# Latent and cross attention by features: values as the held operand, probabilities scaled before they are turned

## The reference

```python
def causal_block_attention(q, k, v, scale):      # queries in blocks of 128
    s = einsum('bqhmd,bkhmd->bhmqk', q_blk, k) * scale     # masked by position
    p = softmax(s, axis=-1)
    return einsum('bhmqk,bkhd->bqhmd', p, v)

# latent: 8 heads, q and k of 96 features, v of 64; output 512 tokens x 512
y_mla = latent_attention(...) @ w_mla_o[l]
# cross: 4 heads of 128 features over 256 memory rows, no mask; output 512 x 512
y_mem = memory_cross_attention(xq, mem_n, ...) @ w_cross_o[l]
merged = gates[:, :, 0] * y_diff + gates[:, :, 1] * y_mla + gates[:, :, 2] * y_mem
x = x + merged @ w_out[l]
```

## Time and profile before

| | us |
|---|---|
| median of 3 runs (3521.92 to 3522.84) | 3522.53 |
| the profiled execution, its own time | 3525.09 |
| its span in the trace | 3523.8 |
| mean share of the TensorE clock granted | 0.981 |

### The profile page before, as it was taken

One profiled execution on the slowest core, in us unless ns is written; L12 is line 12 of the kernel. 1 busy time (PEld: TensorE's weight loads), 2 busy tenths in 40 slices (PEclk: granted clock), 3 DMA queues, 4 the chain that ended last, 5 costly groups with the idle time before them and its releaser, 6 DMA issues.

```text
span 3523.8 us, 53214 instructions
## 1 busy us (share of the span) xinstructions
PE 3367.1 (96%) x21944; PEld 2751.0 (78%) x21944; DVE 2067.1 (59%) x3837; ACT 1332.9 (38%) x2476; POOL 82.7 (2%) x60
## 2 busy tenths in 40 slices
PE   7989999999999999999999999999899989999998
PEld 6777788888888777788888888767677767788887
DVE  6776753554447776644644458655666579664344
ACT  4465543332225566443333223222333234232221
POOL 0000000000000000000000000000000035000000
PEclk9999999999999999999999999999899999999999
DMA  4221223333333221223333333324310324243332
GB/s 137 79 68 49 58 75 108 97 95 96 96 107 119 79 67 49 60 76 116 94 98 96 96 102 89 90 76 118 106 32 28 109 72 138 92 130 96 96 99 86
DMA packets 353816, 314.73 MB, mean 89 GB/s; under 512 B 11348, under 2 KB 281812, under 8 KB 353576
## 3 DMA queue, kind: packets, MB, share of 16 engines
q1 hardware_dynamic: 352712, 309.10, 29.4%
q10 hardware_dynamic: 864, 2.23, 0.2%
HBM read 287.69 MB, written 23.59 MB: 88 GB/s over the span
## 4 chain that ended last, share of the span: by engine, by line
PE 77%; DVE 14%; ACT 4%; issue 3%; DMA 1%; SPq 0%; POOL 0%; DVEq 0%; ACTq 0%; POOLq 0%
PE banks L528 13%; PE banks L530 12%; PE banks L529 12%; PE banks L427 9%; PE banks L429 8%; PE banks L428 8%; DVE weights_r L368 2%; PE banks L628 1%; PE banks L1100 1%; PE banks L1113 1%; ACT weights_high_r L361 1%; PE banks L1204 1%; PE banks L2375 1%; PE banks L2671 1%; PE banks L2610 1%
## 5 line engine op out<-in xcount | busy, mean ns | idle before, releaser
L368 DVE TENSOR_TENSOR weights_r<-weights,weights_high_r 128x1024 fp32r<-128x1024 f32 (+3 forms) x520 | 598.9, 1159 | 360.6 <-ACT weights_high_r L361 359.6
L528 PE MATMUL banks<-h_T_hi,weights_high_r 128*128 128x512 f32 (+2 forms) x1904 | 758.9, 399 | 16.6 <-DVE cellsB L3636 5.1
L530 PE MATMUL banks<-h_T_hi,weights_r 128*128 128x512 f32 (+2 forms) x1904 | 736.6, 387 | 0.0
L529 PE MATMUL banks<-h_T_lo,weights_high_r 128*128 128x512 f32 (+2 forms) x1904 | 736.0, 387 | 0.0
L361 ACT ACTIVATE weights_high_r<-weights 128x1024 fp32r<-128x1024 f32 (+3 forms) x520 | 510.7, 992 | 363.7 <-DMA weights<-in_w_mlp 214.0
L528 PEld LDWEIGHTS banks<-h_T_hi,weights_high_r 128*128 128x128 f32 x1904 | 361.1, 190 | 107.4 <-issue 33.8
L530 PEld LDWEIGHTS banks<-h_T_hi,weights_r 128*128 128x128 f32 x1904 | 360.7, 189 | 72.5
L529 PEld LDWEIGHTS banks<-h_T_lo,weights_high_r 128*128 128x128 f32 x1904 | 361.4, 190 | 69.9 <-issue 3.9
L427 PE MATMUL banks<-weights_high_r,h_T_hi 128*128 128x512 f32 (+3 forms) x704 | 291.8, 414 | 10.6 <-ACT cellsX L577 6.0
L429 PE MATMUL banks<-weights_high_r,h_T_lo 128*128 128x512 f32 (+3 forms) x704 | 267.1, 379 | 0.0
L428 PE MATMUL banks<-weights_r,h_T_hi 128*128 128x512 f32 (+3 forms) x704 | 266.7, 379 | 0.0
(11 more groups left out here) (568 smaller groups left out, 5373.2 us busy)
## 6 DMA issues: line engine op xcount, KB each, us to landing
weights<-in_w_in SPq DMA_DIRECT2D x182, 512.0 KB, 3.8
weights<-in_w_mlp SPq DMA_DIRECT2D x128, 512.0 KB, 3.8
weights<-in_ffn_w_in SPq DMA_DIRECT2D x44, 512.0 KB, 3.8
weights<-in_w_out SPq DMA_DIRECT2D x24, 512.0 KB, 3.6
weights<-in_ffn_w_down SPq DMA_DIRECT2D x22, 512.0 KB, 3.7
weights<-in_w_mem_kv SPq DMA_DIRECT2D x16, 512.0 KB, 3.6
weights<-in_w_diff_o SPq DMA_DIRECT2D x16, 512.0 KB, 3.5
weights<-in_w_mla_o SPq DMA_DIRECT2D x8, 512.0 KB, 3.4
```

Source lines behind the costliest of these rows:

```text
L368: ve.e.tensor_tensor(self.part(c.w_raw_r, u), self.part(c.w_raw, u), self.part(c.w_high_r, u).bitcast(F32), ALU.subtract).then_inc(*ve.tel ...
L528: pe.e.matmul(out, lhsT=wh[:, k, :], rhs=hi[k][:, cols], start=(k == 0), stop=False)
L529: pe.e.matmul(out, lhsT=wh[:, k, :], rhs=lo[k][:, cols], start=False, stop=False)
L530: mm = pe.e.matmul(out, lhsT=wl[:, k, :], rhs=hi[k][:, cols], start=False, stop=(k == self.chunks - 1))
```

## The change

`Attention` now makes its output features by tokens. DVE's reciprocal comes one place earlier in its step (before mask and maximum), ACT then scales the probabilities where they lie in SBUF (a new instruction, unit n-2), the transposes move from unit n-3 to n-4, and the values from n-4 to n-5. In the values product the values are held and the turned probabilities move. For `mla` two heads run together: head 2i writes partitions 0 to 63 of a bank, head 2i+1 partitions 64 to 127, each from 64 held columns, chunk by chunk in turn, and the units are reordered so that the two heads of a pair follow one another. A bank (5 or 7 in turn) collects four query blocks, 512 columns; then ACT copies it out as the high part and DVE subtracts for the low part, straight into the operands of the output projection. Scores have three banks (2 to 4) in place of four. `mla` keeps four turned probability tiles (cells C[0:4]) in place of two; the probabilities rotate over five tiles in place of four. `mo turn` and `xo turn` are gone, and what waited for them waits for `mla.done()` and `cross.done()`, whose marks are now DVE's low parts.

```diff
-    def __init__(self, c, tag, units, out, ready, free):
+    def __init__(self, c, tag, units, together, out, pT, ready, free):
...
+        self.all = together * NT
+        self.n = len(units) + 5
+    def values_pe(self, first):
+        c, pe = self.c, self.c.pe
+        f, block = first // self.all, first % self.all // self.together
+        if block == 0:
+            c.fill(self.tag, "values", f, bank=5 + 2 * (f % 2))
...
+        for j in range(chunks):
+            for e, (m, v) in enumerate(some):
+                dim = v[j].shape[-1]
+                mm = pe.e.matmul(bank[e * dim:(e + 1) * dim, block * P:(block + 1) * P], lhsT=v[j], rhs=self.turned(m)[:, j * P:(j + 1) * P],
+                                 start=(j == 0), stop=(j == chunks - 1))
     def pe(self):
...
+            if self.unit(n - 5) and (n - 4) % self.together == 0:
+                pe.wait_ge("emptied", self.tag, "turn", n - 5)
+                self.values_pe(n - 4 - self.together)
             if self.unit(n - 4):
...
-                    mm = pe.e.matmul(bank[:, 0:v[j].shape[-1]], lhsT=c.pT[n % 2][:, j * P:(j + 1) * P], rhs=v[j],
...
+                pe.wait_ge("scaled", self.tag, m)
...
-                bank = c.fill(self.tag, "scores", n, ring="scores")
+                bank = c.fill(self.tag, "scores", n, bank=2 + n % 3)
     def act(self):
...
+            if self.unit(n - 2):
+                m, st, p = n - 2, self.stat(n - 2), c.probs[(n - 2) % 5][:, 0:self.keys(n - 2)]
+                ac.wait_ge("inverse_sum", self.tag, m)
+                ac.wait_ge("exp", self.tag, m)
+                ac.e.activation(p, p, ACT.Copy, scale=st[:, 3:4]).then_inc(*ac.tell("scaled", self.tag, m))
...
-                ac.e.activation(dst, c.slots[(self.tag, "values", m)][:, 0:dst.shape[-1]], ACT.Copy,
-                                scale=self.stat(m)[:, 3:4]).then_inc(*ac.frees(self.tag, "values", m))
...
+            if f is not None:
+                ac.wait_ge("filled", self.tag, "values", f, NT - 1)
+                ac.wait_all(self.free)
+                ac.e.activation(self.out(f)[0], c.slots[(self.tag, "values", f)][:, :], ACT.Copy).then_inc(*ac.tell("turned_high", self.tag, f))
     def dve(self):
...
+            if f is not None:
+                hi, lo = self.out(f)
+                ve.wait_ge("turned_high", self.tag, f)
+                ve.wait_all(self.free)
+                ve.e.tensor_tensor(lo, c.slots[(self.tag, "values", f)][:, :], hi.bitcast(F32),
+                                   ALU.subtract).then_inc(*ve.frees(self.tag, "values", f))
...
-        mo = plain(C[0:4])
+        mo4 = two_parts(E[0:8:2], E[1:8:2])
-                   for h in range(MH) for b in range(NT)]
+                   for pair in range(MH // 2) for b in range(NT) for h in (2 * pair, 2 * pair + 1)]
-        mo_turn = turn("mo turn", mo, 4, P, pair_out(mo4), mla.done(), mla.done(), pair=True)
-        P_.beside(mo_turn, 183, 184.3)
-        xo_turn = turn("xo turn", xo, 4, P, pair_out(xo4), cross.done(), mla_out.done(), pair=True)
-        P_.beside(xo_turn, 284.5, 292)
```

More of the change, by code:

```diff
@@ L1090, in got, with ended, turned @@
         return self.c.slots[(self.tag, "scores", n)][:, 0:self.keys(n)]
+    def ended(self, n):
+        m = n - 5
+        return m // self.all if self.unit(m) and (m + 1) % self.all == 0 else None
+    def turned(self, n):
+        return self.pT[n % len(self.pT)]
+    def values_pe(self, first):
[3 more added lines that the diff above has]
+            c.fill(self.tag, "values", f, bank=5 + 2 * (f % 2))
+        bank = c.slots[(self.tag, "values", f)]
+        some = [(first + e, self.units[first + e][2]) for e in range(self.together)]
+        chunks = len(some[0][1])
+        for j in range(chunks):
[3 more added lines that the diff above has]
+                                 start=(j == 0), stop=(j == chunks - 1))
+        mm.then_inc(*pe.tell("filled", self.tag, "values", f, block))
     def pe(self):
@@ L1119, in act @@
         for n in range(self.n):
[L1120 to L1129 removed]
+            if self.unit(n - 2):
[3 more added lines that the diff above has]
+                ac.e.activation(p, p, ACT.Copy, scale=st[:, 3:4]).then_inc(*ac.tell("scaled", self.tag, m))
+            if self.unit(n - 4):
+                m, keys = n - 4, self.keys(n - 4)
                 ac.wait_ge("filled", self.tag, "turn", m)
[L1131 to L1133 removed]
+                before = m - len(self.pT)
+                if before >= 0:
+                    ac.wait_ge("filled", self.tag, "values", before // self.all, before % self.all // self.together)
+                ac.e.activation(self.turned(m)[:, 0:keys], c.slots[(self.tag, "turn", m)][:, 0:keys],
                                 ACT.Copy).then_inc(*ac.frees(self.tag, "turn", m))
@@ L1150, in dve @@
         for n in range(self.n):
+            if self.unit(n - 2):
+                m, st = n - 2, self.stat(n - 2)
+                ve.wait_ge("exp", self.tag, m)
+                ve.e.reciprocal(st[:, 3:4], st[:, 2:3]).then_inc(*ve.tell("inverse_sum", self.tag, m))
             if self.unit(n - 1):
@@ L1158, in dve @@
                 if m > 7:
-                    ve.wait_ge("emptied", self.tag, "values", m - 8)
+                    ve.wait_ge("scaled", self.tag, m - 8)
                 ve.e.tensor_reduce(st[:, 0:1], got, AX.X, ALU.max, negate=True).then_inc(*ve.tell("top", self.tag, m))
-            if self.unit(n - 2):
-                m, st = n - 2, self.stat(n - 2)
-                ve.wait_ge("exp", self.tag, m)
-                ve.e.reciprocal(st[:, 3:4], st[:, 2:3]).then_inc(*ve.tell("inverse_sum", self.tag, m))
+            f = self.ended(n)
+            if f is not None:
[4 more added lines that the diff above has]
+                                   ALU.subtract).then_inc(*ve.frees(self.tag, "values", f))
             yield
     def done(self):
-        return [("emptied", self.tag, "values", m) for m in range(max(0, len(self.units) - 4), len(self.units))]
+        return [("emptied", self.tag, "values", f) for f in range(len(self.units) // self.all)]
 class DifferenceAttention(Stage):
@@ L1818, in __init__ @@
         kB_turn = turn("kB turn", kB, 4, P, lambda h: kTB[h], kB_norm.done(), mla.done())
-        mo4 = two_parts(E[0:4], E[4:8])
-        mo_turn = turn("mo turn", mo, 4, P, pair_out(mo4), mla.done(), mla.done(), pair=True)
-        P_.beside(mo_turn, 183, 184.3)
         P_.beside(qB_turn, 183.8, 184)
@@ L1828, in __init__ @@
         bias = lambda n: G["b_gate"][:, n * KD:(n + 1) * KD]
-        mla_out = GatedBranch(c, tag("mla out"), mo4, 4, mo_turn.done(), gates(1), bias(1), i["w_mla_o"][l], merged, False,
-                              [*mo_turn.done(), *kB_turn.done(), *gains])
+        mla_out = GatedBranch(c, tag("mla out"), mo4, 4, mla.done(), gates(1), bias(1), i["w_mla_o"][l], merged, False,
+                              [*mla.done(), *kB_turn.done(), *gains])
         P_.products(*mla_out.jobs)
```

51 lines of the change are left out of this document (17 added, 34 removed).

## The result

The changed kernel takes 3550.07 us (median of 3 runs, 3545.69 to 3552.04) against 3522.53: the ratio is 1.0077, with a 95% interval of 1.0063 to 1.0090. It is 27.5 us slower, where the prediction had 10.8 us faster, and outside the range of 3501 to 3529. The profiled execution is the median one, with a span of 3548.5 us at a mean granted clock of 0.979.

The account below looks back on a forecast made before the run. PE, busy 96% of the span, was taken to bound the kernel. Terms of 1.8 + 1.7 + 1.2 + 1.3 - 0.6 = 5.4 us a layer, 10.8 for two, took 3522.5 to 3511.7 us, range 3501 to 3529.

Parts of the forecast that it names:

- What bounds the kernel: Whole kernel: PE, busy 96% of the span, so PE work removed is time won unless PE then waits.
- The two turns: Removing both turns' transposes from PE: 1.8 us gained for xo turn and 1.7 us net for mo turn, a layer.
- xo turn: Cross attention's turn: its 16 transposes come off PE whole, 1.8 us a layer.
- mo turn: Latent attention's turn: 3.1 us of work and waits gone, 1.4 us of new waits, net 1.7 us a layer.
- The values: Latent attention's values: column halves run at once, 16.0 less 8.8 less 5.6 us of excursions; 1.2 us gained a layer taken.
- B: Rival: loads of 64 held columns in the latent values are not hidden, 8 us more in all, 3519.7 us; chance 0.09.
- C: Rival: the latent values' column halves run in turn, that term becoming -7.2 us a layer, 3528.5 us; chance 0.07.
- The waits at kh1 turn: Where kh1 turn meets mla: the 0.86 us wait goes, the longer stays about the same; 1.3 us gained a layer.
- What is added on ACT and DVE: Scalings and low parts on ACT and DVE, mostly hidden: -0.6 us a layer, ends 0 and -16.
- Rival D: Scaling holds up ACT's copies: PE waits 1.0 us before each of 16 values groups a layer, 3542.5 us; chance 0.08.
- The clock: Sign of being wrong: a second half-clock stretch in the latent attention, about 1.7 us for each 3.4 us, in no case.
- The slack of the transposes: Attention pipeline: the transposes' two steps behind the exponential stay two; no PE cost.

Follow-up runs that it names:

- e4: The kernel before with the change applied to the cross attention alone, the latent attention and its turn left as before; 3515.9 us, ratio 0.9984.
- e9: e3 with DVE's reciprocal removed too, so neither scaling nor reciprocal, outputs of latent and cross attention unnormalised; 3516.3 us, ratio 0.9985 to the kernel before.
- e3: e1 without the scaling instruction and ACT's wait for the reciprocal, outputs of both attentions unnormalised; 3524.2 us, ratio 1.0007 to the kernel before.
- e1: The changed kernel with ACT's copy of the turned probabilities put ahead of the scaling; 3532.9 us, ratio 1.0029 to the kernel before.
- e11: The changed kernel with the scaling on GpSimd's queue and the reciprocal back behind mask and maximum; 3528.1 us, ratio 1.0016 to the kernel before.

## Why the prediction was wrong, point by point

**What bounds the kernel.** Right: PE's work and its waits, and nothing else, make the time. The waits were misjudged, not the bound.

**The two turns.** xo turn: right. Its 32 transposes (of the 64 that are gone) left no wait in the cross attention, and e4, with this term of 3.6 us alone, is 5 us faster (2 to 9). mo turn: forecast 1.7 us net a layer. The idle stretches behind the latent attention are 1.67 + 0.25 + 0.73 = 2.65 us where they were 1.87, so with 1.8 us of work gone the net is 1.0 us in layer 0. kB turn's wait for the low part is what was forecast (some 1.6, it is 1.67); the 0.3 us for shorter waits was too much.

**The values.** The mechanism was right and the size too small. Column halves run at once, 0.109 us for two. The excursion costs 0.25 us and not 0.35: the prediction took it from the row halves of the earlier trace rows, where it had the held operand loaded in the open, and here the loads are hidden. The term is 16.0 - 8.8 - 16 x 0.25 = 3.2 us a layer in place of 1.2. With the turns this makes 2 x (3.6 + 3.2) = 13.6 us of work. The account, with the clock taken out, has 15.3 for the changed kernel, 14.7 for e9 (16.4 less 1.7), 12.9 for e3 (17.1 us at the lower level) and 11.7 for e1 (23.9 us). Rivals B and C fall. The rule of the Trainium skill behind B (TensorE: Matmul & The Clock Gate, The mechanism) does not hold for these loads: held columns for one half were loaded while the other half, with the same rows, ran (at 331.02 us of the changed kernel both halves' passes begin, and the next loads of both begin 2 ns behind them).

**The waits at kh1 turn.** Forecast 1.3 us gained a layer. The stretch grew: 0.65 + 0.25 + 3.61 + 0.86 = 5.4 us in layer 0, where it was 2.26, and 4.4 in layer 1 (0.32, 0.25, 3.61, 0.24), where it was 2.64. The prediction had the late piece right, an exponential behind a weight split, and left its price "at about the same size". It asked what PE would wait for, not what ACT's queue now held ahead of it. The kernel before, at the same place, has the copy 0.1 us behind ACT's half of the split, and PE waits 0.43 us for it:

```profile
285.33 1.05 ACT L361 ACTIVATE weights_high_r<-weights 128x1024 fp32r<-128x1024 f32 x1
...
286.48 0.38 ACT L1133 ACTIVATE cellsS<-banks 128x256 f32<-128x256 f32 x1
...
286.91 0.66 PE L1100 MATMUL banks<-cellsM,cellsS 128*128 128x64 f32 x4 [0.43 <-ACT cellsS L1133]
```

After, it stands behind DVE's half too, through the reciprocal.

**What is added on ACT and DVE: the step that failed.** The term was -0.6 us a layer, and measured it is about -16 (half of the 32 us between after and e9; in the first part of the two accounts alone, -13). The prediction had named -16 as this term's far end and left it out of its range. The sentence that fails is "In most steps the reciprocal will be there: DVE's step runs ahead of PE's transposes". It was not there in 23 of 32 steps. The work was too small as well, 32 scalings of 0.56 us on the mean where it put 0.45, but e3 against e1 puts the worth of all of that work, once it stands behind the copy, at some 4 us a layer. That DVE has a third of its time free, and ACT 44 us, says nothing on this: what counts is how late each queue is at one instruction, and the edit tied both queues to each other twice in a step, ACT's scaling to this step's reciprocal and the reciprocal to the last step's exponential. The text named the danger itself (the scaling "can now hold up the copy. Behind ACT stand then the values, and behind these all of PE") and then priced it from shares of busy time.

**Rival D** is what happened, with a chance of 0.08. It gave 1.0 us for each of 16 groups, 16 us a layer; the copies were awaited for 15.9 and 15.2 us, in 12 waits a layer. Its time was 3542.5; the measured 3550.1 is 7.6 above, and the second part is 8.2 us longer, of which D says nothing. The sign that was named for it, PE idle before the values by ACT's copy, is there in 7 places a layer, and 5 more are before the transposes. Its price of 1.0 us a group is no mean of what came: the waits are fewer and longer (1.3 us on the mean, 3.61 the longest).

**The clock.** Named as something that would make the prediction wrong, and there: a second stretch at the lower level in each layer. In the first part it adds 10.3 us at half speed, 5.1 us of time. As in the earlier trace rows, it stands where PE had idled. Against e9, the first part is 26.3 us longer: 20.1 of idle time, and 6.2 of busy time, which the clock accounts for (41.0 us at the lower level, 27.3 in e9). So in these two executions the waits cost about a third more than their own length.

**The slack of the transposes.** The prediction says that their two steps behind the exponential stay two. They are three now (unit n-1 to unit n-4), two behind the scaling. No row here shows an effect of that.

**The sum once more.** Scaling and reciprocal cost 32 us (after against e9): 17 the order of scaling and copy (e1), 8 the rest of the scaling (e1 against e3), 8 the reciprocal (e3 against e9), each rounded. Without them the change gains 5 us, which is what the cross attention alone gives (e4). So the latent part gave nothing that the intervals of some 4 us let one see, though its values save PE 3.2 us a layer. In the first part of the accounts e9 is 3.3 us shorter than e4 (2056.9 and 2060.2), and loses as much again in the second.

**What stays open.** First, what takes most of the latent part's gain in e9, and what makes scaling and reciprocal near twice as dear in the changed kernel as in the kernel before. e9's 6.6 us of new idle time stand before values and transposes that want the copies, before scores that want an exponential (three banks in place of four), and at the low parts behind the latent attention. No run gave the scores their fourth bank back in this form, or parted the pair's values in time. Second, the second part's 8.2 us: the same instructions, in a stretch that varies by 12 us between kernels. Time at the lower clock there went from 101.7 to 106.9 us, 2.6 of the 8.2; its cause wasn't tried.

## What to carry to other kernels

An engine's queue is in order, so price an added instruction by what stands behind it and when its own input comes, never by its duration or the engine's free share: 0.16 us of reciprocal cost 6 us here, and swapping two independent instructions gave back 17. Before adding a wait between two helper engines, write down for one step, at the place where both are latest (a weight split, a norm), who is waiting for whom and what the bounding engine wants next; put what it wants at the head of the step. And try a change first where nothing is late: in the cross attention the same code was worth 5 us, and with the latent one added the whole lost 33 against that.

## What the hardware did that was not expected

- Two column halves of the array, with the same rows, ran plain fp32 passes at once: 128 moving columns in 0.109 us for the pair, starts 7 ns apart, with each pass's load of 64 held columns (0.14 us as recorded) hidden.
- Going from the whole array to column halves and back cost 0.25 us (0.10 in, 0.15 out); the way out is the same within 0.01 us for groups of 4, 8, 12 and 16 passes.
- GpSimd's scaling of probabilities where they lie takes 1.9 (256 columns) to 2.3 times (512) as long as ACT's. By shape, of e11, and the same of ACT in the changed kernel (layer 0):

```profile
L1198 POOL TENSOR_SCALAR probabilities<-probabilities,softmax_stats 128x256 f32<-128x256 f32 x48 | 45.8, 956 | 390.3 <-DVE softmax_stats L1182 390.3
...
L1198 POOL TENSOR_SCALAR probabilities<-probabilities,softmax_stats 128x512 f32<-128x512 f32 x16 | 26.5, 1657 | 19.0 <-DVE softmax_stats L1182 19.0
```
```profile
L1144 ACT ACTIVATE probabilities<-probabilities,softmax_stats 128x512 f32<-128x512 f32 x8 | 5.8, 719 | 7.4 <-DVE softmax_stats L1177 7.4
...
L1144 ACT ACTIVATE probabilities<-probabilities,softmax_stats 128x256 f32<-128x256 f32 x8 | 4.1, 507 | 10.3 <-DVE softmax_stats L1177 10.3
```

The prediction had at most 0.62 us for such a scaling, from a square of 512 columns; it takes 0.72. That by itself is 0.1 us in eight units a layer.
